# A hybrid decoder step on one Trainium2 core: sample states decayed and updated per sample and head in one VectorE instruction, gate products split four and eleven

## The chip, the cores and the metric

One core of one Trainium2 chip runs the whole program as one launch. The metric is the device time of that core in microseconds (us), lower is better. All arrays are float32.

## The reference, cut to what matters

One decoder layer for a prompt of 256 tokens and for 8 sample sequences of 4 tokens, sharing all weights: an input projection, an HGRN2 branch and an RWKV-7 branch side by side, a gated merge, and a mixture of 32 experts (top 4). The changed lines belong to the HGRN2 branch of the samples, the update of the carried states: 8 samples by 4 heads, each a state of 128 x 128.

```python
D_MODEL = 1024; SEQ = 256; DEC_BATCH = 8; DEC_SEQ = 4
H_A = 4; DK_A = 128; DV_A = 128

    def step(S, blk):
        qc, kc, vc, gc = blk
        b = jnp.cumsum(gc, axis=2)
        o = jnp.einsum("bhtk,bhkv->bhtv", qc * jnp.exp(b), S)
...
        b_last = b[:, :, -1]
        S = S * jnp.exp(b_last)[..., None] + jnp.einsum(
            "bhsk,bhsv->bhkv", kc * jnp.exp(b_last[:, :, None] - b), vc)
        return S, o
...
    merged = (jax.nn.sigmoid(gate_a) * (o_a.astype(x.dtype) @ w_branch_a)
              + jax.nn.sigmoid(gate_b) * (o_b.astype(x.dtype) @ w_branch_b))
    x = x + merged @ w_out

    h = moe(rmsnorm(x, norm2_w).reshape(B * T, D_MODEL), router_w, router_b,
            expert_w_gu, expert_b_gu, expert_w_down, expert_b_down)
```

`S * exp(b_last)` is the decay (one factor for each key, that is for each partition of the stored state), and the second term is the update that TensorE computes. `gate_a` and `gate_b` are 16 blocks of 128 columns of the input projection; their products are independent of the recurrent branches.

## The kernel before, in words

**Engines and order.** Each engine runs a list of instructions written out by hand; they meet only at semaphores. `done(ins, name)` raises a semaphore when an instruction is finished, `step(ins, name)` on VectorE raises it and waits for it on the same engine. There is no planner: TensorE runs exactly in the order in which the code issues.

**The stages.** First the input projection (TensorE, up to 145 us), then the sample sequences of the RWKV branch, then the HGRN2 branch: `hgrn_prompt(0, 0)` (the first 128 prompt tokens), `hgrn_sample()`, `hgrn_prompt(1, 2)` (the other 128). Then four rounds `u` of the RWKV branch on the prompt, the branch products and the merge, the output projection, the router, and the experts. The expert weights, 2 MB a transfer, are loaded by SyncE's queue (`w_load`), which waits for TensorE to release slots. While the branches run, the queue waits for `hg_state`, `hg_o_evac`, `ob_done`, `merged` and `wo_done`, which the branches raise.

**Gate products as filler.** The 16 gate blocks are each 8 products of 128x128 by 128x288. `gate(n)` issues the next n of these products; a product shows in the trace as two matmul records. They are placed by hand at points where TensorE would else wait. The count is a running one: `gate_run(KT * WHOLE)` in `hgrn_prompt(1, 2)` issues whatever is left up to 56 products. A block needs its bank free (`pj_evac`, raised by ScalarE's `gate_evac`), and a block starts at every eighth product.

**The samples' HGRN2 states.** `s0h` holds the 32 states, [128 keys, (sample, head, value)]; `s0v` is its view by sample and head. After the sample outputs (`hg_o` 2), TensorE runs for each group g of four samples: `gate((9, 6)[g])`, a wait (g = 0 for `hg_o_evac` 2, g = 1 for `hg_upd` 4, since the same four banks are used again), and four matmuls of 128x512 into banks 4 to 7, one for each head, then `hg_skv`. VectorE meanwhile multiplies all states by their decays (`gam`, lines 2103 to 2107), and then for each group waits for `hg_skv` and adds the four banks (line 2112), raising `hg_upd` once for each head. `gamH` is the tile behind `gam`; column h * 16 + 8 + b is head h, sample b.

**Who waits for the last addition.** `hg_upd` 8 is awaited by `hgrn_prompt(1, 2)` on TensorE (line 795, before the products of line 801 overwrite banks 4 to 7), by ScalarE's `sample_states_out(1)`, which then issues the store of four samples' states, and, being in order, by VectorE's own next instructions, `hg_mask(2, 1)` (line 2076) and `hg_states(1)` (line 2090). `hgrn_prompt(1, 2)` issues in this order: transposes (784), scores (789), `gate(3)`, the wait for `hg_upd` 8, the products of keys and values (801), the wait for `hg_a`, the products of line 807, the remaining gate products, and the products with the states (819). On ScalarE, `sample_states_out(1)` stands in front of three `gate_evac`.

The recurrent step of the prompt, `hg_states`, is already written in the form that the change brings to the samples:

```python
for h in range(HA):
    a, b = (g % 5) * 512 + h * P, ((g + 1) % 5) * 512 + h * P
    i = v.scalar_tensor_tensor(out=sH[:, b:b + P], in0=sH[:, a:a + P], scalar=pc(gamH, h * 16 + g),
                               in1=bank[4 + c][:, h * P:(h + 1) * P], op0=ALU.mult, op1=ALU.add)
step(i, "hg_state")
```

Of the kernel before, what the change touches and what calls it, by code (L numbers as in the profile page):

```python
# [27 lines left out]
P = 128  # L28
# [4 lines left out]
ALU = mybir.AluOpType  # L33
# [10 lines left out]
HA, DA = 4, 128  # L44
# [28 lines left out]
def bcast(ap, shape):  # L73
    return ap.to_broadcast(shape)


def layer_kernel(nc, x_prompt, x_sample, state_hgrn, state_rwkv, state_shift, norm1_w, w_in, hgrn_lb_logits,
# [5 lines left out]
    with ctx:  # L83
# [40 lines left out]
        gamH = take(4 * (NC_P + NB))  # L124
# [42 lines left out]
        gate = [fm[i] for i in (0, 1, 10, 11)]  # L167
# [4 lines left out]
        bank = [ctx.enter_context(nc.psum_tensor(f"bank{i}", [P, 512], F32)) for i in range(8)]  # L172
# [355 lines left out]
        def _(pe):  # L528
# [11 lines left out]
            for h in range(2):  # L540
                i = mm(bank[6 + h][:, :], ones[0:1, :], norm_bc[0:1, h * 512:(h + 1) * 512], start=True, stop=True)
# [8 lines left out]
            for t, (o, n) in enumerate(TILES):  # L550
# [4 lines left out]
                for k in range(KT):  # L555
                    b = bank[2 * t + k // 4] if t < 2 else bank[4]
                    c = (k % 4) * 128 if t < 2 else k * 40
                    i = nc.tensor.transpose(b[:, c:c + rows], xn[0:rows, t, k * P:(k + 1) * P], ident[0:rows, 0:rows])
# [50 lines left out]
            for n in range(11, 15):  # L609
                chunk_ready(n)  # L610
                slot, _ = mix_chunk(n)
                for t in range(2):
                    bank_free(k)
                    for kt in range(KT):
                        i = mm(bank[k % 4][:, 0:CPC], xv[:, kt, P * t:P * (t + 1)], slot[:, kt, :],  # L615
                               start=(kt == 0), stop=(kt == KT - 1))
                    done(i, "pj_done")
                    k += 1
                if n == 14:
# [3 lines left out]
                    for kt in range(KT):  # L623
                        for x, w in enumerate(slots):
                            i = mm(bank[k % 4][NS * x:NS * x + NS, 0:CPC], xv[:, kt, NP_:NT], w[:, kt, :],
                                   start=(kt == 0), stop=(kt == KT - 1), skip_group_check=True)
# [13 lines left out]
            for q in range(4):  # L640
                pe.wait_ge(S("g_evac"), q + 1)
                for b in range(4):
                    i = nc.tensor.transpose(bank[4 + q][:, b * P:(b + 1) * P], S_s[:, b * 512 + q * P:b * 512 + (q + 1) * P], ident)
# [19 lines left out]
            def gate(n):  # L663

                gate_run(gate_m[0] + n)
# [158 lines left out]
            def hgrn_sample():  # L824

                gate(2)
                pe.wait_ge(S("hg_o_evac"), 1)
                for h in range(HA):
                    i = mm(bank[2][NS * h:NS * h + NS, 0:P], f4(kt_, h, NP_, NS), ident, start=True, stop=True)
                done(i, "hg_kT")  # L830
                for h in range(HA):
                    i = mm(bank[3][NS * h:NS * h + NS, 0:NS], f4(kh, h, NP_, NS), f4(qh, h, NP_, NS),
                           start=True, stop=True)
                done(i, "hg_scores")
                gate(1)
                pe.wait_ge(S("hg_state"), 4)
                pe.wait_ge(S("hg_kT_evac"), 2)
                pe.wait_ge(S("hg_a"), 2)
                for h in range(HA):
                    r = slice(NS * h, NS * h + NS)  # L840
                    mm(bank[4][r, 0:P], aT[r, 0:NS], hi_s[r, :], start=True, stop=False, skip_group_check=True)
                pe.wait_ge(S("s0h_loaded"), 16)
                for b in range(NB):
                    for h in range(HA):
                        i = mm(bank[4][NS * h:NS * h + NS, 0:P], qm[:, h * NT + NS * b:h * NT + NS * b + NS],
                               s0h[:, (b * HA + h) * P:(b * HA + h + 1) * P], start=False, stop=(b == NB - 1),
                               skip_group_check=True)
                done(i, "hg_o")
                pe.wait_ge(S("vexp"), 1)
                for g in range(2):  # L850
                    gate((9, 6)[g])
                    if g:
                        pe.wait_ge(S("hg_upd"), 4)
                    else:
                        pe.wait_ge(S("hg_o_evac"), 2)
                    for h in range(HA):
                        r = slice(NS * h, NS * h + NS)
                        i = mm(bank[4 + h][:, :], ktT[r, 0:P], vexp[r, g * 512:(g + 1) * 512], start=True, stop=True)
                    done(i, "hg_skv")
# [12 lines left out]
            for u in range(4):  # L872
# [39 lines left out]
                for x, (s0, s1) in enumerate(((At, Bn), (Kn, vR))):  # L912
                    if x:
                        pe.wait_ge(S("rw_lower"), u + 1)
                    for q in range(2):
                        for y, src in enumerate((s0, s1)):
                            i = nc.tensor.transpose(bank[2 + x][:, y * 256 + q * P:y * 256 + (q + 1) * P], f4(src, 2 * G + q, o, P), ident)
# [37 lines left out]
                for hh in range(4):  # L955
                    i = mm(bank[7][:, hh * 64:(hh + 1) * 64], PM[:, hh * 512 + 256:hh * 512 + 384],
                           vT[:, t * 512 + (4 * G + hh) * 64:t * 512 + (4 * G + hh + 1) * 64], start=True, stop=True)
# [14 lines left out]
                if u:  # L972
                    g, rows = GATED[u - 1], TILES[GATED[u - 1]][1]
                    pe.wait_ge(S("oa_done"), 3 * u)
                    pe.wait_ge(S("ob_rstd"), u + 1)
                    for q in range(4):
                        i = nc.tensor.transpose(bank[3][:, q * P:q * P + rows], oH[0:rows, g * 512 + q * P:g * 512 + (q + 1) * P],
                                                ident[0:rows, 0:rows])
# [8 lines left out]
                for hh in range(4):  # L987
                    i = mm(bank[7][64 * (hh % 2):64 * (hh % 2) + 64, (hh // 2) * P:(hh // 2 + 1) * P],
                           wta[:, hh * P + 64:(hh + 1) * P], PM[:, hh * 512 + P:hh * 512 + 256], start=True, stop=True)
                done(i, "rw_R")  # L990

                for hh in range(4):
                    out = bank[2][64 * (hh % 2):64 * (hh % 2) + 64, (hh // 2) * P:(hh // 2 + 1) * P]
                    h = 4 * G + hh
# [7 lines left out]
                for hh in range(4):  # L1002
                    h, s, hp = 4 * G + hh, 64 * (hh % 2), hh // 2
# [7 lines left out]
                    for r, out_phi, out in chunks:  # L1011
                        i = mm(out, bnT[r, h64], wta[r, hh * P:hh * P + 64], start=False, stop=False, skip_group_check=True)
# [3 lines left out]
                for c in range(4):  # L1016
                    g = 4 * t + c
# [3 lines left out]
                    for hh in range(4):  # L1021
                        s, hp = 64 * (hh % 2), hh // 2
                        q = 2 * G + hp
                        i = mm(bank[4 + c][s:s + 64, P + hp * 64:P + (hp + 1) * 64],
                               phi[s:s + 64, c * P + hp * 64:c * P + (hp + 1) * 64],
                               s_all[s:s + 64, g * 256 + q * 64:g * 256 + (q + 1) * 64], start=False, stop=True,
                               skip_group_check=True)
                    done(i, "rw_chain")

                    for hh in range(4):  # L1030
                        s, hp = 64 * (hh % 2), hh // 2
                        q = 2 * G + hp
                        i = mm(bank[2][s:s + 64, hp * P + C * c:hp * P + C * c + C],
                               s_all[s:s + 64, g * 256 + q * 64:g * 256 + (q + 1) * 64],
                               Rh[s:s + 64, hp * P + C * c:hp * P + C * c + C], start=False, stop=True,
                               skip_group_check=True)
# [4 lines left out]
            for br in range(2):  # L1041
# [6 lines left out]
                for j in range(KT):  # L1048
# [5 lines left out]
                    for kt in range(4):  # L1054
                        slot, _ = mix_chunk(N_IN + 2 * br + kt // 2)
                        i = mm(bank[n % 2][:, 0:NT], slot[:, kt % 2, j * P:(j + 1) * P],  # L1056
                               (obT if br else oaT)[:, kt * NT:(kt + 1) * NT], start=(kt == 0), stop=(kt == 3))
                    done(i, "branch")
                    if n == 1:
                        pe.wait_ge(S("rw_state"), 16)  # L1060
                        for q in range(4):
                            i = nc.tensor.transpose(bank[4][0:64, q * P:(q + 1) * P],
                                                    s_all[:, 8 * 256 + q * 64:8 * 256 + (q + 1) * 64], ident)
# [180 lines left out]
            for q in range(2):  # L1244
                i = nc.tensor.transpose(bank[6][:, q * P:(q + 1) * P], xg[:, q * P:(q + 1) * P], ident)
# [3 lines left out]
            for q in range(2):  # L1249
                i = nc.tensor.transpose(bank[1][:, q * P:(q + 1) * P], xg[:, (2 + q) * P:(3 + q) * P], ident)  # L1250
# [166 lines left out]
            for x, c in enumerate((slice(0, 256), slice(256, 512))):  # L1417
                pe.wait_ge(S("y_evac"), last * 8 + 8 + x)
                pe.wait_ge(S("xn_done"), XX + 2 + x)
                for h in range(2):  # L1420
                    i = add_part(0, h, c)
# [482 lines left out]
        def _(dve):  # L1904
            v = nc.vector

            def step(ins, name="dve_step"):
                done_wait(dve, ins, name)

            def pc(a, c):  # L1910
                return a[:, c:c + 1]
# [5 lines left out]
            for t, (o, n) in enumerate(TILES):  # L1917
                dve.wait_ge(S("rstd"), t + 1)
                for h in range(2):
                    c = slice(h * 512, (h + 1) * 512)  # L1920
                    i = v.scalar_tensor_tensor(out=xn[0:n, t, c], in0=xs[0:n, t, c], scalar=stat[0:n, 8 + t:9 + t],
                                               in1=bank[6 + h][0:n, :], op0=ALU.mult, op1=ALU.mult)
# [13 lines left out]
            for k in range(14):  # L1936
# [9 lines left out]
                                       in1=es[:, :, 1:5], op0=ALU.mult, op1=ALU.add)  # L1946
                step(v.scalar_tensor_tensor(out=dst[:, 0:NP_], in0=shD[:, 0:NP_], scalar=pc(par, k), in1=e[:, 1:257],
                                            op0=ALU.mult, op1=ALU.add), "shift_done")
# [3 lines left out]
            for q in range(4):  # L1952
                i = v.tensor_scalar(quarter(fm[9], q), quarter(fm[1], q), pc(par, 22 + q), None, ALU.mult)
# [15 lines left out]
            for q in range(4):  # L1969
                i = v.tensor_scalar(quarter(fm[5], q), quarter(fm[4], q), pc(par, 26 + q), pc(omka, q), ALU.mult, ALU.add)  # L1970
# [3 lines left out]
            for q in range(4):  # L1974
                i = v.scalar_tensor_tensor(out=quarter(z1, q), in0=quarter(fm[0], q), scalar=pc(par, 30 + q),
                                           in1=quarter(fm[1], q), op0=ALU.mult, op1=ALU.mult)
# [50 lines left out]
            for s, n in enumerate((C, TS)):  # L2027
                a = chunks(fm[9])[s]
# [72 lines left out]
            dve.wait_ge(S("hg_o"), 2)  # L2101
            v.memset(s_all[:, 0:256], 0.0)
            for g in range(2):
                for h in range(HA):
                    a = s0v[:, 4 * g:4 * g + 4, h, :]
                    i = v.tensor_tensor(a, a, bcast(gam[:, h, 8 + 4 * g:12 + 4 * g].unsqueeze(2), [P, 4, P]), ALU.mult)
            step(i)
            for g in range(2):
                dve.wait_ge(S("hg_skv"), g + 1)
                for h in range(HA):  # L2110
                    a = s0v[:, 4 * g:4 * g + 4, h, :]
                    step(v.tensor_tensor(a, a, bank[4 + h].rearrange("p (b v) -> p b v", b=4), ALU.add), "hg_upd")
            hg_mask(2, 1)
            hg_states(1)
            def heads(a, t, n, h=HB):
# [526 lines left out]
```

## Time and profile before

| what | us |
|---|---|
| median of 3 runs | 1316.17 (1315.21 to 1316.23) |
| the profiled execution, its own time | 1315.27 |
| its span, first to last instruction | 1313.5 |
| TensorE matmul busy | 1284.6 (98%) |
| VectorE busy | 372.6 (28%) |
| ScalarE busy | 241.7 (18%) |
| GpSimd busy | 56.6 (4%) |
| moved by DMA | 449.40 MB, 342 GB/s over the span |

The profile is of one execution. A busy share is an average over stages with different limits; the stage that the change touches lies between 185 and 200 us, and the experts begin at about 407 us. Matmuls are pipelined and their ends are modelled, so that the records of consecutive groups overlap a little.

### The profile page before, as it was taken

The page shows a single profiled execution, that of the slowest core. Times are in us where ns is not written, and L with a number is a line of the kernel's source. Part 1 is how long each engine was busy: PE and PEld are TensorE (multiplying, and loading weights), DVE is VectorE, ACT ScalarE, POOL GpSimd, SP SyncE. Part 2 cuts the span into 40 slices and gives each one's busy share as a digit, 9 for nine tenths or more (in the row PEclk, how much of TensorE's full clock was granted, in tenths as well). Part 3 has the DMA queues.
Part 4 walks back from the last instruction along what each step waited for, and adds up shares of the span by engine and source line. Part 5 has one row for each costly group of instructions (what it writes and reads, how often), then busy time and mean ns, then how long its engine had stood idle before and what let it go on. Part 6 is the DMA issues. An engine that isn't in the chain of part 4 may idle for free.

```text
span 1313.5 us, 18378 instructions
## 1 busy us (share of the span) xinstructions
PE 1284.6 (98%) x7361; PEld 614.0 (47%) x7361; DVE 372.6 (28%) x1016; ACT 241.7 (18%) x532; POOL 56.6 (4%) x131
## 2 busy tenths in 40 slices
PE   9999999999999999999999999999999999999997
PEld 6778778888744333333333333333333333233333
DVE  3234756554327121121221211212112111211112
ACT  3144343222122110111111110111101101110102
POOL 5000200000060000000000000000000000000000
PEclk9999999999999999999999999999999999999999
DMA  7635437111879999999999999999999999999996
GB/s 237 171 99 192 132 84 271 38 33 34 311 276 380 427 430 429 428 429 428 429 428 428 430 429 431 430 429 428 430 430 430 430 430 428 430 431 429 430 428 268
DMA packets 73252, 449.40 MB, mean 342 GB/s; under 512 B 14408, under 2 KB 43130, under 8 KB 47884
## 3 DMA queue, kind: packets, MB, share of 16 engines
q1 hardware_dynamic: 67462, 445.45, 82.9%
q10 hardware_dynamic: 5734, 3.14, 0.8%
q8 instruction: 42, 0.69, 0.2%
q14 instruction: 14, 0.11, 0.0%
HBM read 443.82 MB, written 4.76 MB: 342 GB/s over the span
## 4 chain that ended last, share of the span: by engine, by line
PE 83%; DMA 12%; DVE 2%; ACT 2%; issue 1%; ACTq 0%; SPq 0%; DVEq 0%
PE bank L1289 27%; PE bank L1310 14%; DMA arena<-in_expert_w_gu_dram 7%; PE bank L568 7%; PE bank L1204 5%; PE bank L658 5%; DMA ring<-in_expert_w_gu_dram 5%; PE bank L1235 5%; PE bank L1082 2%; PE bank L1056 2%; PE bank L949 2%; ACT arena L1434 1%; PE bank L1211 1%; PE bank L1279 1%; PE bank L932 1%; PE bank L615 1%
## 5 line engine op out<-in xcount | busy, mean ns | idle before, releaser
L1289 PE MATMUL bank<-ring,arena 128*64 128x512 f32 x1040 | 233.6, 594 | 5.0 <-DMA ring<-in_expert_w_gu_dram 5.0
L1434 ACT ACTIVATE arena<-bank 128x512 f32<-128x512 f32 (+7 forms) x233 | 115.1, 514 | 479.2 <-PE bank L1310 196.2
L1289 PE MATMUL bank<-arena 128*64 128x512 f32 x768 | 173.3, 594 | 2.4 <-DMA arena<-in_expert_w_gu_dram 2.4
L1434 ACT ACTIVATE arena<-arena 128x256 f32<-128x256 f32 (+7 forms) x124 | 68.9, 564 | 468.6 <-DVE arena L2395 461.1
L1289 PEld LDWEIGHTS bank<-ring,arena 128*64 128x64 f32 x1040 | 72.8, 137 | 146.3 <-issue 122.6
L2395 DVE TENSOR_SCALAR arena<-bank 128x256 f32<-128x256 f32 x64 | 26.9, 421 | 375.1 <-PE bank L1289 375.1
L1310 PE MATMUL bank<-ring,arena 128*64 128x512 f32 x544 | 121.9, 595 | 0.0
L2441 DVE COPY arena<-bank 64x512 f32<-64x512 f32 x30 | 20.8, 694 | 318.5 <-PE bank L1310 318.5
L1289 PEld LDWEIGHTS bank<-arena 128*64 128x64 f32 x768 | 53.9, 137 | 105.8 <-issue 92.6
L1204 PE MATMUL bank<-arena 128*64 128x512 f32 x372 | 89.6, 599 | 0.0
L568 PE MATMUL bank<-arena,ring 128*128 128x296 f32 (+1 forms) x352 | 87.6, 411 | 0.0
L1310 PE MATMUL bank<-arena 128*64 128x512 f32 x352 | 79.8, 596 | 0.0
L568 PEld LDWEIGHTS bank<-arena,ring 128*128 128x128 f32 x352 | 66.7, 190 | 19.9
L658 PE MATMUL bank<-arena,ring 128*128 128x288 f32 x256 | 75.5, 419 | 0.0
L1310 PEld LDWEIGHTS bank<-ring,arena 128*64 128x64 f32 x544 | 37.8, 137 | 70.6 <-issue 69.3
L1235 PE MATMUL bank<-arena 128*32 128x256 f32 (+1 forms) x252 | 66.3, 491 | 0.0
L1289 PE MATMUL bank<-extra,arena 128*64 128x512 f32 x240 | 54.2, 593 | 0.7 <-DMA extra<-in_expert_w_gu_dram 0.7
L1204 PEld LDWEIGHTS bank<-arena 128*64 128x64 f32 x372 | 23.8, 134 | 60.6 <-issue 60.6
L1434 ACT ACTIVATE ring<-bank 128x512 f32<-128x512 f32 (+8 forms) x94 | 31.9, 382 | 95.1 <-PE bank L568 50.5
L658 PEld LDWEIGHTS bank<-arena,ring 128*128 128x128 f32 x256 | 44.0, 190 | 10.7 <-issue 2.4
L1310 PEld LDWEIGHTS bank<-arena 128*64 128x64 f32 x352 | 24.3, 137 | 45.1 <-issue 45.0
L1235 PEld LDWEIGHTS bank<-arena 128*32 128x32 f32 (+1 forms) x252 | 24.7, 148 | 34.4 <-issue 34.4
(374 smaller groups left out, 1128.0 us busy)
## 6 DMA issues: line engine op xcount, KB each, us to landing
ring<-in_expert_w_gu_dram SPq DMA_DIRECT2D x63, 2048.0 KB, 23.3
arena<-in_expert_w_gu_dram SPq DMA_DIRECT2D x47, 2048.0 KB, 23.0
ring<-in_expert_w_down_dram SPq DMA_DIRECT2D x35, 2048.0 KB, 23.2
arena<-in_expert_w_down_dram SPq DMA_DIRECT2D x21, 2048.0 KB, 24.3
extra<-in_expert_w_gu_dram SPq DMA_DIRECT2D x15, 2048.0 KB, 25.3
ring<-in_w_in_dram SPq DMA_DIRECT2D x23, 1024.0 KB, 5.4
extra<-in_expert_w_down_dram SPq DMA_DIRECT2D x6, 2048.0 KB, 25.6
ring<-in_w_out_dram SPq DMA_DIRECT2D x4, 1024.0 KB, 7.5
```

Of the source, the lines that this page charges most:

```text
L568: i = mm(b[:, 0:cols], slot[:, kt, j * P:(j + 1) * P], xv[:, kt, 0:cols], start=(kt == 0), stop=(kt == KT - 1))
L658: i = mm(bank[g % 2][:, 0:NT], slot[:, kt, (g % 2) * P:(g % 2 + 1) * P], xv[:, kt, 0:NT], start=(kt == 0), stop=(kt == KT - 1))
L949: i = mm(bank[6 - 4 * x][:, (hh % 2) * P:(hh % 2 + 1) * P], Pm, (zaT if lev > 3 else yaT)[:, hh * P:(hh + 1) * P], start=True, stop=True)
L1056: i = mm(bank[n % 2][:, 0:NT], slot[:, kt % 2, j * P:(j + 1) * P], (obT if br else oaT)[:, kt * NT:(kt + 1) * NT], start=(kt == 0), stop=( ...
L1082: i = mm(out, mT[:, kt * NT + o:kt * NT + o + rows], slot[:, kt % 2, c], start=(kt == 0), stop=True, skip_group_check=True)
L1204: i = mm(bank[6][64 * h:64 * h + 64, :], sel[0:rows, t * SLOTS:(t + 1) * SLOTS], x2[0:rows, t, h * 512:(h + 1) * 512], start=(t == 0), sto ...
L1235: return mm(out, GT[:, o:o + rows], yo[:, c], start=False, stop=True, skip_group_check=True)
L1289: ins = mm(bank[q % 2][64 * (q // 2):64 * (q // 2) + 64, :], gu_lhs(c), w[:, q * 512:(q + 1) * 512], start=(c == 0), stop=(c == KT - 1), s ...
L1310: ins = mm(b[64 * h:64 * h + 64, :], lhs(j, r), w[:, r * D + h * 512:r * D + (h + 1) * 512], start=(j == 0 and r == 0), stop=(j == DN - 1 ...
L1434: return nc.scalar.activation(out, in_, f, **kw)
L2395: v.tensor_scalar(by_row(glu, b), gu_half(b, 0), LIMIT, None, ALU.min).then_inc(S("glu_ready"), 1)
L2441: v.tensor_copy(yo[64 * x:64 * x + 64, 512:1024], bank[1][64:128, :]).then_inc(S("y_evac"), 1)
```

## The change

The eight multiplications of 128x512 by the decays are removed. Each of the eight additions of 128x512 becomes four instructions `scalar_tensor_tensor` on 128x128, one for each sample of the group, that multiply the state by its decay (one number for each partition) and add the product from the bank in one pass, in place; `hg_upd` is still raised once for each head. In front of the two groups of products TensorE issues 4 and 11 gate products instead of 9 and 6; the sum, 15, is the same.

```diff
@@ -848,7 +848,7 @@
                 done(i, "hg_o")
                 pe.wait_ge(S("vexp"), 1)
                 for g in range(2):
-                    gate((9, 6)[g])
+                    gate((4, 11)[g])
                     if g:
                         pe.wait_ge(S("hg_upd"), 4)
                     else:
@@ -2101,15 +2101,13 @@
             dve.wait_ge(S("hg_o"), 2)
             v.memset(s_all[:, 0:256], 0.0)
             for g in range(2):
-                for h in range(HA):
-                    a = s0v[:, 4 * g:4 * g + 4, h, :]
-                    i = v.tensor_tensor(a, a, bcast(gam[:, h, 8 + 4 * g:12 + 4 * g].unsqueeze(2), [P, 4, P]), ALU.mult)
-            step(i)
-            for g in range(2):
                 dve.wait_ge(S("hg_skv"), g + 1)
                 for h in range(HA):
-                    a = s0v[:, 4 * g:4 * g + 4, h, :]
-                    step(v.tensor_tensor(a, a, bank[4 + h].rearrange("p (b v) -> p b v", b=4), ALU.add), "hg_upd")
+                    for b in range(4):
+                        a = s0v[:, 4 * g + b, h, :]
+                        i = v.scalar_tensor_tensor(out=a, in0=a, scalar=pc(gamH, h * 16 + 8 + 4 * g + b),
+                                                   in1=bank[4 + h][:, b * P:(b + 1) * P], op0=ALU.mult, op1=ALU.add)
+                    step(i, "hg_upd")
             hg_mask(2, 1)
             hg_states(1)
```

## Rows read from the trace of the kernel before

**Rows 1.** The page: TensorE's granted clock (tenths) and DMA load in 40 slices

```profile
PEclk9999999999999999999999999999999999999999
DMA  7635437111879999999999999999999999999996
```

**Rows 2.** Waits of TensorE: us in total, times, longest us

```profile
PE bank L1289 <- DMA ring<-in_expert_w_gu_dram: 5.0, 6, 1.2
...
PE bank L541 <- DMA arena<-in_norm_w_dram: 2.5, 1, 2.5
```

**Rows 3.** The same from 160 to 400 us, the only two

```profile
PE bank L1056 <- DVE arena L2161: 0.4, 1, 0.4
PE bank L801 <- DVE ring L2112: 0.2, 1, 0.2
```

**Rows 4.** Windows: busy us, granted clock, DMA share, GB/s

```profile
core 0: us, PE busy (x) PEld busy (x) DVE busy (x) ACT busy (x) POOL busy (x), PEclk, DMA share, GB/s
...
386.00:390.00 4.00, 4.00 (x23) 2.45 (x22) 1.39 (x2) 1.47 (x3) 3.92 (x2) 1.00 0.01 2
...
1000.00:1260.00 260.00, 245.72 (x1144) 82.74 (x1140) 48.60 (x162) 30.30 (x58) 0.00 (x0) 1.00 1.01 430
1304.00:1313.00 9.00, 2.69 (x14) 0.96 (x14) 4.22 (x8) 4.68 (x16) 2.83 (x2) 0.84 0.35 131
```

**Rows 5.** Timeline, TensorE, 184 to 201 us: start, length, line, count, wait before

```profile
184.98 4.63 PE L658 MATMUL bank<-arena,ring 128*128 128x288 f32 x18
189.55 1.14 PE L858 MATMUL bank<-ring 32*128 32x512 f32 x8
190.62 3.18 PE L658 MATMUL bank<-arena,ring 128*128 128x288 f32 x12
193.73 1.14 PE L858 MATMUL bank<-ring 32*128 32x512 f32 x8
...
196.19 1.62 PE L658 MATMUL bank<-arena,ring 128*128 128x288 f32 x6
198.01 1.17 PE L801 MATMUL bank<-arena,ring 32*128 32x128 f32 x32 [0.20 <-DVE ring L2112]
199.11 1.16 PE L807 MATMUL bank<-arena,ring 128*128 128x128 f32 x8
```

**Rows 6.** Timeline, VectorE, 174 to 198 us

```profile
174.74 4.59 DVE L2090 SCALAR_TENSOR_TENSOR ring<-ring,arena,bank 128x128 f32<-128x128 f32 x16 [0.48 <-PE bank L801]
...
185.46 4.83 DVE L2106 TENSOR_TENSOR ring<-ring,arena 128x512 f32<-128x512 f32 x8
190.82 2.85 DVE L2112 TENSOR_TENSOR ring<-ring,bank 128x512 f32<-128x512 f32 x4 [0.53 <-PE bank L858]
195.01 2.85 DVE L2112 TENSOR_TENSOR ring<-ring,bank 128x512 f32<-128x512 f32 x4 [1.33 <-PE bank L858]
197.89 0.69 DVE L2076 TENSOR_TENSOR ring<-bank,arena 128x512 f32<-128x512 f32 x1
```

**Rows 7.** Line 2090: the first five, the first six, and the length of one

```profile
174.74 1.50 DVE L2090 SCALAR_TENSOR_TENSOR ring<-ring,arena,bank 128x128 f32<-128x128 f32 x5 [0.48 <-PE bank L801]
...
174.74 1.76 DVE L2090 SCALAR_TENSOR_TENSOR ring<-ring,arena,bank 128x128 f32<-128x128 f32 x6 [0.48 <-PE bank L801]
...
L2090 DVE SCALAR_TENSOR_TENSOR ring<-ring,arena,bank x32: 339/342/349, 174.7 to 203.5; 128x128 f32<-128x128 f32 x32
```

**Rows 8.** Timeline, ScalarE and its DMA issues; time of these stores to landing

```profile
185.28 1.11 ACT L1434 ACTIVATE ring<-bank 32x128 f32<-32x128 f32 x4
...
193.77 0.42 ACTq L1621 DMA_DIRECT2D out_dram<-ring  x1
...
197.89 1.36 ACTq L1621 DMA_DIRECT2D out_dram<-ring  x1
199.35 0.71 ACT L1434 ACTIVATE arena<-bank 128x288 f32<-128x288 f32 x2 [3.26 <-issue]
...
DMA to landing us min/median/max: 10.0/10.0/10.1
```

## The prediction

> **What bounds the kernel now.** I read the page first. TensorE's clock is granted in full in all 40 slices, and from the slice that begins at 394 us to the last but one the DMA engines are 90% busy or more [rows 1]. The windows say it closer: from 1000 to 1260 us the DMA share is 1.01 at 430 GB/s, while TensorE is busy 245.72 of 260 us; the last stretch in which the DMA engines do nothing is 386 to 390 us, share 0.01 [rows 4]. So the end is set by a stream of expert weights that never stops once it has started. What starts it are releases by the branches, the merge and the output projection. The question is then what bounds the branches. The waits of TensorE answer it: its waits for the expert loads of line 1289 are 1.2 us at most [rows 2], and from 160 to 400 us there are only two, 0.4 us for line 2161 and 0.2 us for line 2112 [rows 3]. None is for a DMA. In the branches, then, TensorE goes through its own list without a pause, the gate products filling every hole, and a new pause anywhere in it moves everything behind it, the start of the weight stream included. VectorE's load is of no interest as such; only the moments at which TensorE asks for its results are.
>
> The 0.2 us belong to the very place of the change: the products of line 801 wait for the last addition of line 2112. TensorE's `gate(3)` ends at 196.19 + 1.62 = 197.81 us, and line 801 starts at 198.01 us [rows 5]; the last addition ends at 195.01 + 2.85 = 197.86 us [rows 6]. From the end of the addition to the start of the products it is 0.15 us. VectorE is thus already the one that comes last here, by a hair: there is no slack behind which longer additions could hide.
>
> **The change, part by part.**
>
> *The eight multiplications go.* They take 4.83 us from 185.46 us and end 0.53 us before VectorE gets its first products [rows 6]. They lie beside nine gate products on TensorE [rows 5]; nobody waits for them. Removing them at the old split is worth nothing.
>
> *The split 4 and 11.* It moves five gate products from in front of the first group of products to behind it; no instruction is added, no DMA moved. Eighteen matmul records (nine products) span 189.55 - 184.98 = 4.57 us, 0.508 us a product [rows 5]; four take 2.03 us. The first group so starts at 184.98 + 2.03 = 187.01 us instead of 189.55. The wait in front of it, for the copies of the sample outputs, is met: ScalarE ends them at 185.28 + 1.11 = 186.39 us [rows 8]. The group takes 190.62 - 189.55 = 1.07 us, and the eleven products at the pace of the six (193.73 - 190.62 = 3.11 us, 0.518 each) take 5.70 us. TensorE asks for `hg_upd` 4 at 187.01 + 1.07 + 5.70 = 193.78 us, against 193.73 before; I take the same time, since the same 15 products and one group lie in front of it. Eight-product boundaries fall at the same running counts, and the bank releases of ScalarE that they need are not nearer than before. The split alone moves no end.
>
> *The additions become 16 instructions for each group.* The price stands in the trace, in the prompt's own recurrence: the same operation, shape, operands (bank, two tensors, a scalar for each partition), the same semaphore after every fourth. Sixteen take 4.59 us from the first start to the last end [rows 6]. Five take 1.50 and six 1.76 us, so one more within a four costs 0.26 us; with 0.34 us the length of one, the five hold 1.50 - 0.34 = 1.16 us of starts, of which 3 x 0.26 = 0.78 are inside a four and 0.38 is the step over the semaphore [rows 7]. The old form took 2.85 us for a group [rows 6]. A group so costs 4.59 - 2.85 = 1.74 us more. That the result is written over its input I cost at nothing; the old additions did it too.
>
> The Trainium skill speaks against this part of the change: "VectorE: DVE Perf Modes", section "The TRN2 errata", has it that a fixed cost is paid for every instruction on SBUF operands, and advises tiles of at least 512 elements. The rows agree in direction: four instructions of 128 cost 1.16 us where one of 512 costs 2.85 / 4 = 0.71 us [rows 6, 7].
>
> *Group 0 lies beside work.* From the start of the products to VectorE's start it is 190.82 - 189.55 = 1.27 us [rows 5, 6]. VectorE starts at 187.01 + 1.27 = 188.28 and ends at 192.87 us. TensorE asks at 193.73: 0.86 us to spare, covered by the eleven gate products. Without that cover (the old 9 and 6) the end would be 195.41, a wait of some 1.7 us here too. ScalarE issues the first store 0.8 us earlier; nobody waits for it then.
>
> *Group 1 lies on the path.* Its products start at 193.73 as before, VectorE at 195.01. It ends at 195.01 + 4.59 = 199.60 instead of 197.86 us. Between them and line 801 TensorE has the transposes, the scores and three gate products, up to 197.81 us as before, and nothing was moved there. Line 801 starts at 199.60 + 0.15 = 199.75 instead of 198.01: the wait of 0.2 us becomes 1.9 us, **+1.74 us**.
>
> *What is queued behind.* On VectorE, the mask of line 2076 (0.69 us) and the recurrence of line 2090, which wait for line 801 anyway; the mask is ready 0.69 us after the additions, and line 807, 1.1 us behind line 801, still finds it [rows 5, 6]. On ScalarE, the second store is issued 1.74 us later, and behind its issue (1.36 us) stand the evacuations of gate blocks at 199.35 us [rows 8]; the next gate block starts 1.1 us behind line 807, and both sides of that move by 1.74 us together. The stores land 10.0 us after issue [rows 8]; what waits for them moves too. On SyncE, the expert loads behind `hg_state` 8 move with it.
>
> *Does anything give it back?* It would take a later wait of TensorE for something that doesn't move. From 200 to 400 us the one wait, 0.4 us, is for VectorE [rows 3], which moves; every release of a weight transfer in that stretch comes from TensorE, VectorE or ScalarE. Behind 400 us the transfers lie back to back. I find nothing.
>
> **The sum:** 0 (multiplications) + 0 (split) + 0 (group 0) + 1.74 (group 1) = +1.7 us. The profiled execution took 1315.27 us (span 1313.5); with it, 1317.0. The median of the runs shown is 0.9 us above that execution, and I state the forecast against the median: 1316.17 + 1.74 = **1317.9 us**, 0.13% above before.
>
> Bounds of the one price that matters: at the fastest pitch, 0.26 us throughout, a group takes 15 x 0.26 + 0.34 = 4.24 us, +1.4. At the slowest step, 0.38 us throughout, 15 x 0.38 + 0.34 = 6.04 us, +3.2 in group 1, and group 0 would end at 194.3, 0.6 us too late: +3.8. I take 4.59, measured on the same form with the same semaphores.
>
> **The rivals.** The bound for telling it from no change is 0.2%, 2.6 us.
>
> *Slower (the other side):* the instructions do not overlap as in line 2090 but run end to end at 0.34 us each. Sixteen then take 5.5 us; group 1 adds 2.6 us, and group 0 ends at 193.75, just in time: 1318.8. What could do it is the one difference of form, the result written over the input. Against it speaks that line 2112 writes over its input, at 0.71 us for 512 elements. It decides only above 0.34 us each. The Trainium skill has a rule of this kind ("VectorE: DVE Perf Modes", "The DRAIN you can't avoid"): the next VectorE operation waits until the pipeline has emptied. Line 2090's starts, 0.26 us apart at a length of 0.34, don't show it in full [rows 7].
>
> *Slower, by the clock:* TensorE pauses for 1.9 us in a stretch where it never did. The clock falls where TensorE is mostly idle: 0.84 in the last 9 us, with 2.69 us busy [rows 4]. If it fell to 1.2 GHz for the work from line 801 to line 819 (some 8 us), that would cost up to 8 us: 1326. Against it: the wait of 2.5 us at the start left the clock at full [rows 1, 2].
>
> *No cost, or faster:* the wait comes but is taken back, by a slack in the DMA stream that the waits don't show, or TensorE's earlier start of group 0 helps something. That gives 1316.2; to be faster it would have to shorten the stream itself, and the only wait it could remove is worth 0.2 us: 1316.0.
>
> **How the numbers follow.** A pause of 1.4 to 2.2 us that passes to the end, within 0.2%: 0.77. Taken back in part or whole: 0.08, within 0.2% as well. Slower instructions, or a delay added behind the pause, over 2.6 us: 0.09. The clock: 0.03. Faster by over 0.2%: 0.03, for what I can't see. Together faster 0.03, same 0.85, slower 0.12. The range takes in the case taken back, less half the spread of the runs, 1315.9, and the slow pitches up to 1319.4, short of their far end (1320.0) and of the clock.
>
> **What the profile after would show.** Line 858's groups at about 187.0 and 193.7 us. VectorE: 16 instructions in 4.6 us from 188.3 and from 195.0, nothing from 185.6 to 188.3. No wait of TensorE at the second group. Line 801 at about 199.75 with a wait for the fused line of some 1.9 us. All behind it, the first expert product too, later by 1.7 us, DMA share 1.01 as before. The forecast is wrong if the sixteen take other than 4.6 us, if the second group waits, or if the experts' start moves by 1.7 us and the end does not.

## The result, and the profile after

| | median, us | runs |
|---|---|---|
| before | 1315.56 (1314.96 to 1316.23) | 11 |
| after | 1319.05 (1317.56 to 1319.98) | 11 |

The ratio is 1.0025, with an interval of 1.0017 to 1.0033: the changed kernel is slower, by 3.5 us. That is inside the stated range (1315.9 to 1319.4), but just beyond the 0.2% that the forecast took as its likeliest side, and twice the 1.74 us that it summed. That it lies inside is partly luck. The range was built on 1316.17 us, the median of three runs; built on the 1315.56 of the eleven it would end at 1318.8. And its top stood for slow instructions on VectorE, which did not come. The runs after fall into two groups: four from 1317.56 to 1318.22 us and seven from 1318.97 to 1319.98. Their mean granted clocks are 0.998 or 0.999 in the first group and 0.997 or 0.998 in the second. The profiled execution (1319.40 us, span 1317.6, clock 0.997) is of the second.

TensorE's timeline after, as [rows 5]; the columns are start, length, line, operation, count of records, and in brackets the wait before it:

```profile
185.08 2.21 PE L658 MATMUL bank<-arena,ring 128*128 128x288 f32 x8
187.22 1.14 PE L858 MATMUL bank<-ring 32*128 32x512 f32 x8
188.29 5.60 PE L658 MATMUL bank<-arena,ring 128*128 128x288 f32 x22
193.82 1.14 PE L858 MATMUL bank<-ring 32*128 32x512 f32 x8
...
196.28 1.62 PE L658 MATMUL bank<-arena,ring 128*128 128x288 f32 x6
199.85 1.52 PE L801 MATMUL bank<-arena,ring 32*128 32x128 f32 x32 [1.95 <-DVE ring L2108]
201.30 2.08 PE L807 MATMUL bank<-arena,ring 128*128 128x128 f32 x8
203.17 4.43 PE L658 MATMUL bank<-arena,ring 128*128 128x288 f32 x16
207.52 2.46 PE L819 MATMUL bank<-ring,arena 128*32 128x128 f32 x32
```

VectorE's, as [rows 6], and two rows from further on:

```profile
188.43 4.60 DVE L2108 SCALAR_TENSOR_TENSOR ring<-ring,arena,bank 128x128 f32<-128x128 f32 x16 [2.78 <-PE bank L858]
195.10 4.60 DVE L2108 SCALAR_TENSOR_TENSOR ring<-ring,arena,bank 128x128 f32<-128x128 f32 x16 [2.08 <-PE bank L858]
199.73 0.69 DVE L2076 TENSOR_TENSOR ring<-bank,arena 128x512 f32<-128x512 f32 x1
...
226.81 0.42 DVE L2189 TENSOR_TENSOR ring<-arena,bank 128x256 f32<-128x256 f32 x1 [0.40 <-DVE ring L2189]
...
283.07 0.42 DVE L2189 TENSOR_TENSOR arena<-arena,bank 128x256 f32<-128x256 f32 x1 [0.38 <-DVE arena L2189]
```

The middle of the forecast is there to a tenth of a microsecond. The first group of products (line 858) starts at 187.2 us, the second at 193.8 us without a wait; sixteen fused instructions take 4.60 us, twice; VectorE ends at 199.70 us, and line 801 starts at 199.85 us behind a wait of 1.95 us. This trace runs 0.09 us late throughout, so line 801 is 199.85 - 198.01 - 0.09 = 1.75 us later than before.

What was not forecast stands in the next rows. Line 801 takes 1.52 us instead of 1.17, line 807 2.08 instead of 1.16, the sixteen records of line 658 4.43 us instead of 4.05 in the same place before. Line 819 starts 3.44 us later than before (207.52 against 204.08). Windows of one microsecond say why; the columns are those of [rows 4]:

```profile
198.00:199.00 1.00, 0.00 (x0) 0.00 (x0) 0.96 (x5) 0.00 (x0) 0.00 (x0) 1.00 1.14 349
199.00:200.00 1.00, 0.15 (x4) 0.18 (x8) 0.97 (x4) 0.00 (x0) 0.00 (x0) 1.00 1.15 349
200.00:201.00 1.00, 1.00 (x32) 1.00 (x31) 0.42 (x1) 0.71 (x2) 0.00 (x0) 0.76 1.14 350
201.00:202.00 1.00, 1.00 (x11) 0.78 (x7) 0.59 (x3) 0.00 (x0) 0.00 (x0) 0.50 1.08 376
202.00:203.00 1.00, 1.00 (x7) 1.00 (x7) 0.96 (x5) 0.00 (x0) 0.00 (x0) 0.50 1.00 348
203.00:204.00 1.00, 1.00 (x4) 0.84 (x4) 0.96 (x5) 0.00 (x0) 0.00 (x0) 0.53 1.09 364
204.00:205.00 1.00, 1.00 (x5) 0.76 (x4) 0.96 (x5) 0.00 (x0) 0.00 (x0) 1.00 1.13 351
```

TensorE does nothing from 197.9 to 199.8 us. Within the microsecond from 200 us its granted clock goes down, to 0.50, which is its level of 1.2 GHz; from 204 us it is full again. In the trace before it is 1.00 in all these microseconds. Between line 801 and line 819 this costs 3.44 - 0.09 - 1.75 = 1.60 us.

The rest of the difference comes at two moments, line 658 behind the first round's second squaring (227.84 against 224.10 us: +3.74) and again in the third round (286.42 against 282.34: +4.08). The two rows before, then the two after:

```profile
224.10 2.59 PE L658 MATMUL bank<-arena,ring 128*128 128x288 f32 x10
282.34 0.65 PE L658 MATMUL bank<-arena,ring 128*128 128x288 f32 x2
...
227.84 2.59 PE L658 MATMUL bank<-arena,ring 128*128 128x288 f32 x10
286.42 0.65 PE L658 MATMUL bank<-arena,ring 128*128 128x288 f32 x2
```

In front of both stands one of VectorE's two rows above with a wait for VectorE itself, 0.40 and 0.38 us: the instruction before it has ended, nothing else is awaited, and it does not start. Before, there are no such waits in this stretch. Together they cost 0.64 us, 4.08 - 3.44.

From there everything moves by the same 4.1 us. SyncE issues the first transfer of the last start of the weight stream at 395.81 us instead of 391.72, and then the stream is as it was, against [rows 4]:

```profile
1000.00:1260.00 260.00, 246.37 (x1150) 83.32 (x1148) 48.62 (x162) 30.29 (x58) 0.00 (x0) 1.00 1.01 429
```

In this execution 1.75 + 1.60 + 0.64 = 4.0 us, and the span is 4.1 us longer.

### The profile page after: what moved, and what is told of

Same layout as the page of the kernel before. It is cut to its first block, busy times and chain, and to the rows that moved or that the text cites. A ratio compares the mean times of both kernels' runs of the same rounds, so it can differ in the third digit from the quotient of the medians.

```text
span 1317.6 us, 18393 instructions
## 1 busy us (share of the span) xinstructions
PE 1286.7 (98%) x7361; PEld 615.6 (47%) x7361; DVE 373.5 (28%) x1032; ACT 241.6 (18%) x532; POOL 56.5 (4%) x131
## 4 chain that ended last, share of the span: by engine, by line
PE 83%; DMA 12%; DVE 2%; ACT 2%; issue 1%; ACTq 0%; SPq 0%; DVEq 0%
PE bank L1289 27%; PE bank L1310 14%; DMA arena<-in_expert_w_gu_dram 7%; PE bank L568 7%; PE bank L1204 5%; PE bank L658 5%; DMA ring<-in_expert_w_gu_dram 5%; PE bank L1235 5%; PE bank L1082 2%; PE bank L1056 2%; PE bank L949 2%; ACT arena L1434 1%; PE bank L1211 1%; PE bank L1279 1%; PE bank L932 1%; PE bank L615 1%
```

## The experiments

Ten kernels, each timed in turn with the kernel before on the same chip; "before" is the median of those runs, 1315.7 to 1315.9 us. Theory A: the cost is the pause of TensorE in front of line 801, with the fall of the clock behind it. Theory B: the two short waits of VectorE come with the place of its instructions in its program, that is with how many instructions stand in front of them.

**The split alone.** The kernel before with this edit:

```diff
-                    gate((9, 6)[g])
+                    gate((4, 11)[g])
```

> The old VectorE instructions with the gate products split 4 and 11: the first half of the change's cost is taken out. Theory A (the cost is a pause of TensorE in front of line 801 and what follows from it): the split alone costs nothing, 0 us against before, ratio 1.000, granted clock 0.999; line 858 groups at 187.0 and 193.7 us, VectorE adds to group 0 later than the multiplications end, line 801 at 198.0 us. Rival (the split itself disturbs something, as the bank releases of ScalarE): +0.5 us or more.

Measured: 1315.65 us, ratio 1.0002 (0.9992 to 1.0011). TensorE, second group of products and line 801:

```profile
193.75 1.14 PE L858 MATMUL bank<-ring 32*128 32x512 f32 x8
...
198.03 1.17 PE L801 MATMUL bank<-arena,ring 32*128 32x128 f32 x32 [0.20 <-DVE ring L2112]
```

The split moves group 0 by 2.4 us and the end by nothing, as priced.

**The fused form with the old split.** The changed kernel with this edit:

```diff
-                    gate((4, 11)[g])
+                    gate((9, 6)[g])
```

> The fused instructions with the old split 9 and 6: the second half of the change alone. By the working of the prediction, group 0's instructions now end at 190.82 + 4.59 = 195.4 us against TensorE's request at 193.7: a wait of 1.7 us in front of line 858's second group, and the wait of 1.9 us in front of line 801 as in the changed kernel. Theory A with the clock: +1.7 +1.74 + 0.65 (VectorE's short waits) = +4.1 us at full clock, up to 1.6 more behind each pause where the clock falls, so +4.1 to +7.3. Rival (the split is what costs, the fused form is harmless): at most +1 us.

Measured: 1319.93 us, ratio 1.0030 (1.0021 to 1.0040), +4.0 us; six of nine runs from 1319.45 to 1320.32 us, three from 1321.34 to 1321.52. The waits of TensorE (us in total, times, longest) from 150 to 400 us, and the clock, of an execution of the upper group:

```profile
PE bank L801 <- DVE ring L2108: 1.9, 1, 1.9
PE bank L858 <- DVE ring L2108: 1.6, 1, 1.6
...
200.00:202.00 2.00, 0.65 (x13) 0.68 (x17) 1.86 (x6) 0.26 (x1) 0.00 (x0) 0.88 0.64 163
202.00:204.00 2.00, 2.00 (x30) 1.78 (x24) 0.64 (x3) 0.45 (x2) 0.00 (x0) 0.50 1.07 368
204.00:206.00 2.00, 2.00 (x11) 1.81 (x10) 1.93 (x8) 0.00 (x0) 0.00 (x0) 0.76 1.14 347
```

Without its cover group 0 costs 1.7 us, as the prediction said: the second group starts at 195.33 us instead of 193.73, in a trace that runs 0.08 us early. The four and eleven do what they are for: they hide group 0, and only group 0. Behind the first pause the clock stayed full in this execution, behind the second it fell. The two groups of runs are 1.6 us apart here too (medians 1319.87 and 1321.48).

**Group 0 fused, group 1 as before,** split 4 and 11. The VectorE part of the changed kernel becomes:

```diff
+            for h in range(HA):
+                a = s0v[:, 4:8, h, :]
+                i = v.tensor_tensor(a, a, bcast(gam[:, h, 12:16].unsqueeze(2), [P, 4, P]), ALU.mult)
+            step(i)
...
+            dve.wait_ge(S("hg_skv"), 2)
+            for h in range(HA):
+                a = s0v[:, 4:8, h, :]
+                step(v.tensor_tensor(a, a, bank[4 + h].rearrange("p (b v) -> p b v", b=4), ALU.add), "hg_upd")
```

> Split 4 and 11; group 0 in the fused form, group 1 as before (four multiplications ahead, in the time in which VectorE would wait for group 0's products, then four additions of 512). Theory A: group 0 was priced at nothing, so line 801 starts at 198.0 us behind a wait of 0.2 us, clock full, 0 us against before; with eight instructions more on VectorE the two short waits may stay or go, 0 to +0.65. Rival (the fused form costs wherever it stands): +1.7 or more.

Measured: 1315.83 us, ratio 0.9998 (0.9989 to 1.0007). Line 801 starts at 198.00 us behind a wait of 0.20 us, as before, the clock is 0.999, and neither short wait of VectorE is there. The whole loss is group 1 and what hangs on the rest of the change: the pause, the clock, and 15 records more in VectorE's program (8 more here).

**The pause without the fused form.** The kernel before, split 4 and 11, with two VectorE products that no result uses:

```diff
                 dve.wait_ge(S("hg_skv"), g + 1)
+                if g:
+                    v.tensor_tensor(vexp, vexp, vexp, ALU.mult)
+                    v.tensor_tensor(aT, aT, aT, ALU.mult)
```

> The kernel before with the split 4 and 11 and with two unneeded VectorE products (1024 and 512 elements, some 1.8 us, their results are used by nobody) in front of the second group's additions: the pause of TensorE without any fused instruction. Theory A with the clock: line 801 at 199.8 us behind a wait of some 2 us, then the half clock for 3 us: +1.8 + 1.6 = +3.4 us when it falls, +1.8 when it doesn't; no short waits of VectorE at 226 and 283 us if these come with the place of its instructions. Rival (the fused form is what costs): +1.8 at most and a full clock.

Measured: 1317.51 us, ratio 1.0019 (1.0010 to 1.0028); six runs from 1316.88 to 1317.51 us and five from 1318.39 to 1319.06. The profiled execution is of the lower group. TensorE:

```profile
199.76 1.17 PE L801 MATMUL bank<-arena,ring 32*128 32x128 f32 x32 [1.94 <-DVE ring L2115]
200.86 1.16 PE L807 MATMUL bank<-arena,ring 128*128 128x128 f32 x8
201.85 4.05 PE L658 MATMUL bank<-arena,ring 128*128 128x288 f32 x16
```

The same pause as in the changed kernel, 1.94 us, moves the rest by 1.75 us and no more, when the clock stays full: the three rows have their lengths of before. The two groups of runs are some 1.6 us apart (medians 1317.36 and 1318.95), which is what the half clock cost in the trace of the changed kernel, and the upper group has the lower mean clocks (0.997 or 0.998 against 0.998 or 0.999). No run of the upper group was profiled for this kernel, so that its clock fell at this place is inferred. The fused form is not needed for either; what it costs is the time that it takes.

**The pause filled.** The changed kernel with products of the identity and ones in front of the wait, into a bank that line 807 writes anew:

```diff
                 if t:
+                    keep_busy(7, bank[2])
                     pe.wait_ge(S("hg_upd"), 8)
```

> The changed kernel with seven extra 128x128 products of ones (their result is used by nobody) where TensorE waits 1.95 us for line 801; the wait's end is the same. Theory A with the clock: the pause as such costs 1.74 us and the half clock behind it another 1.6 us in the profiled execution; with the pause filled, the granted clock stays at full, line 801 starts at the same time, and the total falls from +3.5 to about +2.4 us against before (1.74 and the two short waits of VectorE, 0.65). Rival (the slow products from 200 to 204 us come from memory traffic or from VectorE's instructions reading the banks, not from the pause): the products of lines 801, 807 and 658 stay as slow and the total stays at +3.5.

Measured: 1318.15 us, ratio 1.0020 (1.0011 to 1.0029), +2.4 us, all eleven runs in one group (1317.39 to 1319.01), clocks 0.998 or 0.999. TensorE (line numbers are one higher than in the changed kernel):

```profile
197.57 1.72 PE L547 MATMUL bank<-arena 128*128 128x128 f32 x14
199.58 1.17 PE L802 MATMUL bank<-arena,ring 32*128 32x128 f32 x32 [0.29 <-DVE ring L2109]
200.69 1.16 PE L808 MATMUL bank<-arena,ring 128*128 128x128 f32 x8
201.68 4.05 PE L658 MATMUL bank<-arena,ring 128*128 128x288 f32 x16
```

The wait ends within 0.1 us of when it did, but the products behind it run at full speed, though VectorE reads the same banks and the same transfers are in flight: the slow products came from the pause. What is left is 2.4 us by the medians. This trace, which runs 0.08 us early, has 1.65 for the pause and 0.63 for VectorE's two short waits, which are still there. The same kernel with **three** products instead of seven:

> The changed kernel with three extra products of ones instead of seven in the pause in front of line 801: some 0.8 us of the 1.95 are filled, 1.2 us stay idle, the wait's end is the same. Theory A with the clock: as with seven, +2.4 us; if the clock falls in a few executions at this length of pause, those lie 1.6 us higher (about 1319.7), fewer of them than in the changed kernel (7 of 11). Rival (any pause of over 1 us here costs the half clock as often as 1.95 us does): median +3.5 as in the changed kernel.

Measured: 1318.04 us, ratio 1.0020 (1.0011 to 1.0030), with the wait at

```profile
199.79 1.17 PE L802 MATMUL bank<-arena,ring 32*128 32x128 f32 x32 [1.19 <-DVE ring L2109]
```

Ten of eleven runs lie from 1317.40 to 1318.74 us. The eleventh took 1322.59 us at a mean clock of 0.995; it was not profiled, so where its clock fell isn't known. By the grouping of the times, an idle gap of 1.2 us so leaves the clock alone in ten runs of eleven, one of 1.95 us in four of eleven (after) or six of eleven (the pause alone).

**VectorE's instructions moved in its program.** The kernel before with 15 tiny instructions, put where VectorE is idle for 3.9 us:

```diff
             hg_mask(2, 1)
             hg_states(1)
+            for x in range(15):
+                v.memset(vexp[:, x:x + 1], 0.0)
```

> The kernel before with 15 one-column memsets on VectorE behind line 2090's second run, where VectorE is idle for 3.9 us: everything behind them sits 15 instructions later in VectorE's program, as in the changed kernel, and nothing else differs. Theory B (the 0.4 us waits of VectorE at 226 and 283 us, with nothing awaited, come with the place of its instructions in the program): the two waits are there and the total is +0.6 us. Rival (they follow from the shifted times or from the data in flight): no such waits, 0 us.

Measured: 1316.41 us, ratio 1.0005 (0.9996 to 1.0014), +0.7 us. The interval includes no change; the trace shows the two waits, in the same two places (columns: us in total, times, longest), from 200 to 340 us:

```profile
DVE ring L2193 <- DVE ring L2193: 0.4, 1, 0.4
DVE arena L2193 <- DVE arena L2193: 0.4, 1, 0.4
```

Against before, TensorE's line 658 moves by 0.26 us behind the first and by 0.59 us behind both. Counted from zero over all of VectorE's records in the trace, waits on semaphores included, the late starts are at records 319 and 447 here, in the changed kernel and in the filled one: the same numbers, 128 apart, though the kernels differ in front of them. In the kernels before, with the split alone and with group 0 fused, other instructions stand at these numbers, and they start on time. So the place matters, and it is not the only condition.

A third place shows in the kernel with the pause alone, which has only 2 records more than before: its record 575, again 128 further on. Here is that instruction, and under it the same instruction before:

```profile
352.57 0.46 DVE L2233 TENSOR_TENSOR arena<-bank,arena 128x288 f32<-128x288 f32 x1 [1.34 <-PE bank L1056]
...
350.46 0.46 DVE L2230 TENSOR_TENSOR arena<-bank,arena 128x288 f32<-128x288 f32 x1 [0.99 <-PE bank L1056]
```

It starts 0.35 us late, and nothing is lost by it: the weight stream starts 1.75 us later than before (393.47 against 391.72 us), which is the pause alone.

What has a period of 128 is the loading of the program itself. The page has two DMA queues of the kind "instruction"; the columns are packets, MB and share:

```profile
q8 instruction: 42, 0.69, 0.2%
q14 instruction: 15, 0.12, 0.0%
```

A packet of q14 has 8 KB. In the trace of the changed kernel one starts at 227.46 us and one at 283.73 us, both 0.7 us behind a late start (226.81 and 283.07); in the kernel with 15 memsets they start at 224.17 and 280.45 us, again 0.7 us behind (223.51 and 279.75). But with group 0 fused one follows record 447 just so (281.86 behind 281.19 us), and there nothing was late. That VectorE moves on to a new block of its program at these places is thus well supported; why that costs time in some kernels and not in others stays open.

With 16 memsets on top of the filled kernel (the same edit, 16 for 15):

> The changed kernel with the pause filled by seven extra products (as in the earlier run) and 16 one-column memsets on VectorE behind line 2090, in idle time: its later instructions sit another 16 places further on. Theory B (the two waits of 0.4 us come with the place in the program): they leave the two spots, and the total is the pause alone, +1.7 us instead of +2.4; or, if the new places also fall on instructions that TensorE waits for, other such waits show elsewhere. Rival (every added instruction brings such a wait, wherever it is): two or more remain, +2.4 or more.

Measured: 1318.16 us, ratio 1.0016 (1.0007 to 1.0025), +2.25 us. The wait is again at record 319, but that is now another instruction, a step earlier in the same round; the one at 447 no longer shows. One wait fewer should be worth 0.3 us; 1318.16 against 1318.15 in the other session, each against its own before, cannot tell that. The two traces can. Against the filled kernel this one is 1.36 us late at the second group of products (195.01 against 193.65 us), a delay from the very start of the program, and only 1.05 us late at the start of the weight stream (394.98 against 393.93 us): 0.31 us less. So the waits do go by the place in the program, and they did not all leave.

**Trying to win the pause back.** The changed kernel with two gate products moved from the groups to the place in front of the pause:

```diff
-                    gate((4, 11)[g])
+                    gate((3, 10)[g])
...
                 if t:
-                    gate(3)
+                    gate(5)
```

> The fused instructions in both groups, with the gate products split 3, 10 and 5: two taken from in front of the groups and put between the scores and the wait for the last addition. The groups start at 186.5 and 192.8 us, the fused instructions end at 198.65, line 801 starts at 198.8 us behind a wait of 0.9 us instead of 1.95. Theory A: +0.8 us and 0.65 for the short waits, +1.4 in all, and the shorter pause leaves the clock full in all executions (no second cluster 1.6 us higher). Rival (the clock falls with any pause here, or the cost does not come from the pause): +2.4 or more.

Measured: 1316.84 us, ratio 1.0008 (0.9999 to 1.0017), +0.9 us. TensorE:

```profile
192.68 1.14 PE L858 MATMUL bank<-ring 32*128 32x512 f32 x8
...
198.70 1.17 PE L801 MATMUL bank<-arena,ring 32*128 32x128 f32 x32 [0.97 <-DVE ring L2108]
```

The groups start a microsecond earlier, the wait is 0.97 us, and line 801 is 0.76 us late (0.69, with this trace 0.07 us early). One run of eleven (1319.28 us, clock 0.997) lies apart from the rest (1316.31 to 1317.58). This wins back most of the loss. The same split with **group 0 fused and group 1 as before**:

> Group 0 fused, group 1 in the old form, gate products split 3, 10 and 5: the version that the readings so far point to. The additions of group 1 end at 192.7 + 1.3 + 2.85 = 196.9 us, TensorE asks for them at 197.8 us. Theory A: the last wait of TensorE in this stretch (0.2 us in the kernel before) goes and nothing else changes, so -0.2 us against before, too little for the measurement to tell: ratio 0.9998 to 1.000. Rival (moving gate products behind the scores delays something else): +0.3 or more.

Measured: 1316.09 us, ratio 1.0005 (0.9996 to 1.0014), +0.4 us. The interval includes no change, but the trace speaks for the rival. Line 801 starts 0.28 us earlier without a wait (197.65 us in a trace that runs 0.08 us early), but then TensorE waits elsewhere:

```profile
PE bank L658 <- ACT arena L1434: 0.5, 1, 0.5
```

The next gate block needs a bank that ScalarE empties only after it has issued the store of group 1's states, and this issue takes long here:

```profile
196.83 2.97 ACTq L1621 DMA_DIRECT2D out_dram<-ring  x1
```

It starts 1.06 us earlier than before and takes 2.97 us instead of 1.36 [rows 8]. What makes it long isn't known. No version tried beats the kernel before.

## Why the prediction held where it did, and where it did not

- **Bound and transmission** (a pause in the branches moves the start of a weight stream that never stops): shown. Each pause came out at the end, to within some 0.5 us; the DMA share is 1.01 in both.
- **Multiplications and split at nothing, group 0 at nothing with the eleven products as its cover, 1.7 us without:** shown by the split alone, by group 0 fused alone (both within 0.1 us of before) and by the old split (1.7 us).
- **Sixteen fused instructions at 4.59 us, priced from line 2090:** 4.60. The rival by which they run end to end, 5.5 us, is out, in place or not. The Trainium skill's page "VectorE: DVE Perf Modes", section "The DRAIN you can't avoid", says that the next operation waits until the pipeline has emptied, and adds that one that is not held back starts earlier. This trace agrees with the addition: sixteen of 0.34 us each end after 4.60 us.
- **Group 1 at +1.74 us:** 1.75.
- **The clock.** This is the step that failed. It was a rival at 0.03 with up to 8 us; by the grouping of the times it happened in seven of eleven runs, at 1.6 us. The argument against it was the wait of 2.5 us at the start, behind which the clock is full. That wait is in front of TensorE's very first product, at 2.51 us, and did not speak for a pause between dense stretches. The price was too high, because the clock was back at 204 us, half-way to line 819.
- **The place of VectorE's instructions.** The sum had no term for it: 15 records more were costed only by their durations. They cost another 0.64 us in the trace, 0.3 for each of two starts that came late where TensorE was waiting.
- **The wait that ScalarE's store issue might bring** (1.36 us before): it took 0.40 us after. The long one before came 0.05 us behind an issue by SyncE (197.89 and 197.84 us), but so did the one of the split alone (197.91 and 197.86 us), which took 0.43 us. What sets this time stays open.

The sum, as it should have read: 1.74 + 0.65 = 2.4 us, and another 1.6 in most runs. Measured: 2.1 us in the lower group of runs (median 1317.7), 3.8 in the upper (1319.4), 3.5 over all. The mechanism that was forecast is right and stands for half of the loss.

## What to carry to other kernels

A saving of work on an engine that nobody waits for is worth nothing, and a lengthening of the one result that is awaited with no slack is paid in full: find the instruction at which the bounding engine already waits 0.2 us, and look at what the edit does to that one, whichever engine got less busy. Fewer passes are not fewer instructions: 4 x 128 elements cost 1.16 us where 512 cost 0.71, so a fused form in smaller pieces belongs where filler covers it. A pause of a dense TensorE stretch is priced with the clock in mind, as a chance of so many runs; run times that fall into two groups were its sign here.

## What the runs showed of the hardware that was not expected

TensorE idle for 1.95 us in a dense stretch was granted 1.2 GHz for the products behind the gap, until 204 us, in the profiled execution of the changed kernel; by the grouping of the times the same happened in 7 of 11 runs of it and in 5 of 11 with the pause alone. With the old split a second trace shows such a fall, behind a wait of 1.94 us. Filling the gap with useless products kept the full clock.

VectorE started an instruction late, by 0.4 us, at records 319, 447 or 575 of its program: at the first two in six kernels with 15 records more than before, at 319 alone with 31 more, at 575 alone with 2 more, and at none of them in four others. It costs only where that instruction is awaited. The Trainium skill, "Runtime: NRT & Kernel Launch", section "Instruction fetch mechanics", has each engine's instructions fetched in blocks of 256 and the crossing mostly hidden; the places here are 128 records apart, so this trace does not agree with the 256 for VectorE, and a crossing that is awaited cost 0.3 us. That the late starts are such crossings is argued from the period and from the packets of q14, not shown.
